# Dilated attention: two heads run among the query-key slabs, two among parts of three output slabs

## The chip, the cores and the metric

One Trainium2 chip, one NeuronCore. The time is the device time of one execution in microseconds (us): 1809.47 as the median of 3 runs (1809.37 to 1809.75) of the kernel before.

## What is computed

A two-layer block (x of 256 tokens by 1024, even mixer, odd mixer, each with a gated feed-forward part) and behind it a second two-layer block. The change touches only the odd mixer of the first block:

```python
z = h @ w_in
lru_x, lru_gate, q, k, v = jnp.split(z, [LRU_WIDTH, 2 * LRU_WIDTH, 2 * LRU_WIDTH + DIL_QKV, 2 * LRU_WIDTH + 2 * DIL_QKV], axis=-1)
xc = causal_dwconv(lru_x, lru_conv_w) + lru_conv_b
y_lru = rg_lru(xc, lru_wa, lru_ba, lru_wx, lru_bx, lru_lam) * jax.nn.gelu(lru_gate)
y_att = dilated_attention(q, k, v, q_norm_g, k_norm_g)
return jnp.concatenate([y_lru, y_att], axis=-1) @ w_out
```

`rg_lru` makes two sigmoid gates r and i from xc, a = exp(-8 r softplus(-lam)), the factor sqrt(1 - a*a), and a scan over the tokens. `dilated_attention` has 4 heads of 64 channels and, for each head, 3 patterns of (window, dilation): (128, 1), (512, 4), (2048, 16). Queries and keys are normalised to unit mean square over the 64 channels; the outputs of the 3 patterns are weighted by the softmax of their log-sums, which is one softmax over all the keys of the three patterns together.

## The kernel before

**Slabs.** All large products go through slabs: 256 output channels by 1024 (for the output projection 768) inputs of float32 weight. SyncE loads a slab's two halves into `w_raw` (three slots). ScalarE rounds each half to float32r, `w_hi` (`weights_hi`, L1149), which has three slots too: `done(slab)` (L1160) waits until TensorE has finished a slab and then rounds the slab three ahead into its slot. GpSimd or VectorE forms the rest, `w_lo = w_raw - w_hi` (`split_lo`, L471), two slabs ahead (`SPLIT_AHEAD`). TensorE multiplies in three passes for each 128 inputs: hi times hi, lo times hi, hi times lo (`passes`), 24 matmuls per half of 1024 inputs, 48 per slab, into one of four PSUM banks `lin[number % 4]`. `slab_products` (L696) makes channels by tokens, `slab_tokens` (L721) tokens by channels (for the values). Each engine has its own list of instructions, written out by hand and in order, and they meet only at semaphores.

**The odd mixer.** The order of TensorE is: 4 slabs `od_lru`, 6 slabs `od_qk` (each 128 query and 128 key channels), 3 slabs `od_v`, 4 slabs `od_out` of 768 inputs. A channel chunk of 128 holds two heads of one pattern; the chunks 0, 2, 4 are heads 0, 1 of the three patterns and 1, 3, 5 heads 2, 3.

- Query-key norm, for slab n: ScalarE squares (`qk_square`, L1355), TensorE takes the mean over 64 channels with one float32 matmul of 512 columns (`qk_mean`, L896; it writes all of `stat`, so it waits until root n-1 is out), ScalarE takes the root (`qk_root`, L1364), VectorE the reciprocal and two multiplies that also free the slab's bank (`qk_norm`, L1852). In the list of TensorE, `qk_mean(n-1)` stands behind slab n.
- The recurrence: TensorE makes the gate logits (`lru_gate`, L903) behind slabs 1 and 3, ScalarE the sigmoids, tanh and exp (L1374 to L1385, inside the loop over the slabs), VectorE the products, the scan and the gating (L1868 to L1897).
- Attention runs in 8 units, u = 2 * head + token half (`at_logits`, L927, `at_mask`, L1874, `at_exp`, L1399, and the loops L945 to L980, L1409 to L1424, L1898 to L1910). A unit is: logits (3 matmuls of 64 rows) into `logit`; VectorE scales and masks into `score`, and takes the maximum; ScalarE exp with its sum; VectorE reciprocal and scaling; TensorE 3 or 6 transposes into `tr` (and `stat`); ScalarE copies them to `pt1`; TensorE 3 or 6 value products into a bank of `lin` that is not yet in use; ScalarE copies the result into `acc`. For units 1 to 4 TensorE also lays 6 matmuls of `out_0`, the first output slab, on the recurrence's four chunks ahead of the transposes.
- Behind the last unit ScalarE rounds `acc` (both chunks, L1426), VectorE makes its low part, and TensorE does the last two chunks of out_0 (`late_part`, L760) and the slabs out_1 to out_3 (`closing`, L770). In the loop of the units the transposes and the value products of u stand where the line of dots is:

```python
for u in range(2 * DIL_H):
    if u + 2 < 2 * DIL_H:
        at_logits(u + 2)
    if 1 <= u <= 4:
        late_part(out_0, out_operand, range(k, k + NC4 // 2), OUT_LAST, wait_out_chunk, (half,))
    ...
late_part(out_0, out_operand, range(NC4, OUT_LAST + 1), OUT_LAST, wait_out_chunk)
closing([slab_at("od_out", j) for j in range(1, 4)], out_operand, None)
```

**The residual and the next norm.** As each output slab ends, ScalarE's `residual` (L1181) rounds the slab three ahead, waits for VectorE's add into x (`add_residual`, L1654), writes the gained chunks twice (rounded and not) and their squares; GpSimd's `residual` (L554) splits a half of the slab two ahead, makes the low parts of the first four chunks, and adds squares; VectorE's list has the other split halves and the low parts of the last four chunks. The first slab of the feed-forward part (`gained_products`, L789) starts with those chunks, and `norm_mean` (L741, one mean over all channels) stands behind it; from there the feed-forward slabs follow.

**DMA.** SyncE issues the halves of all slabs in slab order, each when `w_raw`'s slot is free.

## Time and profile before

| | |
|---|---|
| runs, median (lowest to highest) | 1809.47 us (1809.37 to 1809.75) |
| the profiled execution | 1810.56 us |
| its span, first to last instruction | 1808.7 us |
| mean granted TensorE clock | 0.987 |
| TensorE matmul busy | 1731.5 us, 96% of the span |
| VectorE, ScalarE, GpSimd busy | 1362.1, 1020.6, 677.7 us |

How to read it: a row of a timeline has the start from the span's beginning, the duration, the engine, the line, the operation, the names written and read, and how many instructions it merges; in brackets stands the idle time of the engine just before, and what ended it. PE is TensorE's matmul, PEld its weight load, DVE VectorE, ACT ScalarE, POOL GpSimd, SP SyncE. Matmuls overlap in the pipeline: one of 256 columns is drawn 0.28 us long and the next starts 0.12 us after it. The granted clock is the share of 2.4 GHz that TensorE had; 0.5 is 1.2 GHz.

### The profile page before, as it was taken

To read this page: it belongs to the slowest core of one execution; us is meant where nothing else is said; L and a number is where in the kernel's file an instruction comes from. 1 tells how busy PE (TensorE), PEld (TensorE's weight loads), DVE (VectorE), ACT (ScalarE), POOL (GpSimd) and SP (SyncE) were. 2 spreads that over 40 slices of the span, in tenths; PEclk is the share of its full clock that TensorE was granted. 3 is DMA by queue.
4 is the path that set the end of the run, shared out by engine and by line. 5 is a ranking of instruction groups with operands and counts; after the bars stand their busy time and mean duration, and the time that the engine had idled before them with its cause. 6 is when DMAs were issued, how large, how long until landed. Compare 5 with 4: busy or idle time off the path is not lost. (4 is left out here: it accounts for less than half of the span.)

```text
span 1808.7 us, 33606 instructions
## 1 busy us (share of the span) xinstructions
PE 1731.5 (96%) x13858; PEld 1686.1 (93%) x13858; DVE 1362.1 (75%) x1967; ACT 1020.6 (56%) x1571; POOL 677.7 (37%) x417
## 2 busy tenths in 40 slices
PE   6989999997999999999999999999999998999997
PEld 6989999986999999999889999999999888999997
DVE  5758875474686859994779589778997578769794
ACT  5465555673654564576663566546367565366462
POOL 6631104950310265344454501038334355331113
PEclk9999999998999999999999999999999999999999
DMA  7435645531455554454234455555354333545552
GB/s 268 151 112 180 201 166 176 195 114 35 146 188 185 168 189 152 163 182 143 99 125 164 163 174 196 178 176 186 129 176 163 117 116 130 176 152 196 187 173 85
DMA packets 80649, 288.42 MB, mean 159 GB/s; under 512 B 9072, under 2 KB 9328, under 8 KB 80368
## 3 DMA queue, kind: packets, MB, share of 16 engines
q1 hardware_dynamic: 79488, 283.15, 46.8%
q10 hardware_dynamic: 1008, 3.11, 0.5%
q8 instruction: 110, 1.80, 0.4%
q14 instruction: 43, 0.35, 0.1%
HBM read 285.18 MB, written 1.05 MB: 158 GB/s over the span
## 5 line engine op out<-in xcount | busy, mean ns | idle before, releaser
L1157 ACT ACTIVATE w_hi<-w_raw 128x1024 fp32r<-128x1024 f32 (+1 forms) x546 | 538.0, 1033 | 337.0 <-PE lin L677 336.0
L477 POOL TENSOR_TENSOR w_lo<-w_raw,w_hi 128x1024 fp32r<-128x1024 f32 (+1 forms) x198 | 476.9, 2420 | 360.9 <-ACT w_hi L1157 355.2
L675 PE MATMUL lin<-h_hi,w_hi 128*128 128x256 f32 x1952 | 560.6, 287 | 24.3 <-DVE w_lo L477 18.3
L675 PE MATMUL lin<-hid_hi,w_hi 128*128 128x256 f32 x1936 | 553.5, 286 | 10.5 <-DVE hid_lo L486 7.2
L676 PE MATMUL lin<-h_lo,w_hi 128*128 128x256 f32 x1952 | 555.3, 284 | 0.0
L677 PE MATMUL lin<-h_hi,w_lo 128*128 128x256 f32 x1952 | 555.2, 284 | 0.0
L676 PE MATMUL lin<-hid_lo,w_hi 128*128 128x256 f32 x1936 | 548.6, 283 | 0.0
L677 PE MATMUL lin<-hid_hi,w_lo 128*128 128x256 f32 x1936 | 548.5, 283 | 0.0
L477 DVE TENSOR_TENSOR w_lo<-w_raw,w_hi 128x1024 fp32r<-128x1024 f32 (+1 forms) x348 | 495.1, 1426 | 36.9 <-ACT w_hi L1157 35.9
L675 PEld LDWEIGHTS lin<-h_hi,w_hi 128*128 128x128 f32 x1952 | 377.7, 194 | 26.5 <-issue 17.5
L675 PEld LDWEIGHTS lin<-hid_hi,w_hi 128*128 128x128 f32 x1936 | 372.2, 192 | 13.3 <-DVE hid_lo L486 6.1
L676 PEld LDWEIGHTS lin<-h_lo,w_hi 128*128 128x128 f32 x1952 | 377.8, 194 | 0.8 <-issue 0.5
L677 PEld LDWEIGHTS lin<-h_hi,w_lo 128*128 128x128 f32 x1952 | 377.6, 193 | 0.0
L676 PEld LDWEIGHTS lin<-hid_lo,w_hi 128*128 128x128 f32 x1936 | 372.4, 192 | 0.3
L677 PEld LDWEIGHTS lin<-hid_hi,w_lo 128*128 128x128 f32 x1936 | 372.3, 192 | 0.0
L1691 DVE SCALAR_TENSOR_TENSOR acc<-arena,par,acc 128x254 f32<-128x254 f32 (+1 forms) x264 | 156.4, 632 | 3.0
L486 POOL TENSOR_TENSOR h_lo<-arena,h_hi 128x256 fp32r<-128x256 f32 x48 | 36.3, 764 | 279.5 <-ACT h_hi L1215 219.2
L486 POOL TENSOR_TENSOR hid_lo<-arena,hid_hi 128x256 fp32r<-128x256 f32 x48 | 36.3, 762 | 258.6 <-ACT hid_hi L1215 219.2
L1669 DVE TENSOR_TENSOR x<-x,lin 128x512 f32<-128x512 f32 x64 | 43.8, 685 | 100.8 <-PE lin L677 100.8
L1705 DVE TENSOR_TENSOR arena<-lin,std 128x512 f32<-128x512 f32 x88 | 60.7, 690 | 60.5 <-PE lin L677 60.3
L1227 ACT ACTIVATE acc<-arena,par 128x256 f32<-128x256 f32 x88 | 48.3, 596 | 93.8 <-DVE arena L1705 93.8
L1223 ACT ACTIVATE acc<-arena,par 128x256 f32<-128x256 f32 x44 | 26.5, 603 | 112.1 <-DVE arena L1705 112.1
(307 smaller groups left out, 2148.3 us busy)
## 6 DMA issues: line engine op xcount, KB each, us to landing
w_raw<-in_upA SPq DMA_DIRECT2D x112, 512.0 KB, 3.6
w_raw<-in_upB SPq DMA_DIRECT2D x64, 512.0 KB, 4.2
w_raw<-in_xbc SPq DMA_DIRECT2D x48, 512.0 KB, 4.1
w_raw<-in_dnA SPq DMA_DIRECT2D x32, 512.0 KB, 3.5
w_raw<-in_dnB SPq DMA_DIRECT2D x32, 512.0 KB, 3.4
w_raw<-in_z SPq DMA_DIRECT2D x32, 512.0 KB, 4.1
w_raw<-in_gates SPq DMA_DIRECT2D x32, 512.0 KB, 3.8
w_raw<-in_ps SPq DMA_DIRECT2D x32, 512.0 KB, 4.0
```

Source lines behind the costliest of these rows:

```text
L477: eng.tensor_tensor(w_lo[slab.slot][:, half, part], w_raw[slab.slot][:, half, part], w_hi[slab.slot][:, half, part].bitcast(F32), ALU.subt ...
L486: return eng.tensor_tensor(lo, whole, hi.bitcast(F32), ALU.subtract)
L675: nc.tensor.matmul(out, lhs[0], rhs[0], start=first, stop=False)
L676: nc.tensor.matmul(out, lhs[0], rhs[1], start=False, stop=False)
L677: return nc.tensor.matmul(out, lhs[1], rhs[0], start=False, stop=last)
L1157: nc.scalar.activation(w_hi[slab.slot][:, half, part], w_raw[slab.slot][:, half, part], ACT.Copy)\
L1223: nc.scalar.activation(acc[:, b, 0, :], zz[:, j, 0, :], ACT.Identity, bias=pcol(f"fb{f}", c), scale=pcol(f"fw{f}", 2 * FC + c)).then_inc(s ...
L1227: ins = nc.scalar.activation(acc[:, b, i, :], zz[:, j, i, :], ACT.Identity, bias=pcol2(l, "fb", i * FC + c), scale=pcol2(l, "fw", 2 * 2 * ...
L1669: tt(pairs[:, j, :, :], pairs[:, j, :, :], lin[slab.bank][:, :, :], ALU.add)\
L1691: ins = stt(outs[i][:, d:T], ins_[i][:, 0:T - d], weight(taps - 1 - d, i), outs[i][:, d:T], ALU.mult, ALU.add)
L1705: tt(zz[:, j, :, :], lin[slab.bank][:, :, :], std[:, 0, 0:T].unsqueeze(1).to_broadcast([P, 2, T]), ALU.mult).then_inc(s.bank_free[slab.ban ...
```

## The change

The arrays of weights are cut anew: the q-k slabs come in the order of chunks 0, 2, 4, then 1, 3, 5 (`od_qa`, `od_qb`), the values by head pair (`od_va` with head 0, `od_vb` with the others), and between them the order of slabs is `od_qa` 3, `od_va` 1, `od_qb` 3, `od_vb` 2, `od_out` 4. Units 0 to 3 (heads 0, 1) run among the slabs of `od_qb` and `od_vb`, in the middle of a slab too (`between`), with their value products written to `tr`. Units 4 to 7 run among parts of out_0, out_1 and out_2, whose first four chunks are laid between the steps of the units, the chunk of heads 0, 1 next, and the chunk of heads 2, 3 behind the last unit. The lists of ScalarE and VectorE are written out anew to match; the high and low part of the attention's output are made per chunk (`att_round`, `att_rest`). GpSimd splits both halves of out_2. Cut to its core:

```diff
+QK_ORDER = (0, 2, 4, 1, 3, 5)
...
-         ("od_lru", 4), ("od_qk", 6), ("od_v", 3), ("od_out", 4),
+         ("od_lru", 4), ("od_qa", 3), ("od_va", 1), ("od_qb", 3), ("od_vb", 2), ("od_out", 4),
...
+        def at_product(u):
+            lo = 64 * (u // 2 % 2)
+            return (tr if u < UNITS // 2 else lin[slab_at("od_out", 3).bank][:, 0, :])[lo:lo + 64, 0:P]
...
+                    if k < both:
+                        split_lo(pool, slab_at(stage, k, l).ahead(SPLIT_AHEAD), 1)
...
+            residual("od_out", 3, both=1)
...
+            slab_products(qk_slabs[0], h_op(1))
+            stage_released(pe, "od_lru")
+            pe.wait_ge(s.lru_first, 2)
+            lru_gate(0)
+            slab_products(qk_slabs[1], h_op(1))
+            qk_mean(0)
+            pe.wait_ge(s.lru_r, 1)
+            lru_gate(1)
+            slab_products(qk_slabs[2], h_op(1))
+            qk_mean(1)
+            slab_tokens(v_slabs[0], 1, lambda: qk_mean(2))
+            slab_products(qk_slabs[3], h_op(1))
+            at_logits(0)
+            slab_products(qk_slabs[4], h_op(1), between=lambda: at_logits(1))
+            at_transposes(0)
+            qk_mean(3)
+            def first_values():
+                at_values(0)
+                at_logits(2)
+            slab_products(qk_slabs[5], h_op(1), between=first_values)
+            at_transposes(1)
+            def second_values():
+                at_values(1)
+                at_logits(3)
+                qk_mean(4)
+            slab_tokens(v_slabs[1], 1, second_values)
+            at_transposes(2)
+            qk_mean(5)
+            slab_tokens(v_slabs[2], 1)
+            at_transposes(3)
...
+            def out_part(j, chunks, halves=(0, 1)):
+                for half in halves:
+                    if chunks[0] == 0:
+                        outs[j].wait_split(pe, half)
+                        if half == 0:
+                            outs[j].wait_bank_free(pe)
+                    late_part(outs[j], out_operand, chunks, OUT_LAST, wait_out_chunk, (half,))
...
+            out_part(0, from_lru, (0,))
+            at_values(2)
+            out_part(0, from_lru, (1,))
+            at_values(3)
+            at_logits(4)
+            out_part(1, from_lru)
+            at_logits(5)
+            out_part(2, from_lru, (0,))
+            at_transposes(4)
+            out_part(2, from_lru, (1,))
+            at_values(4)
+            at_logits(6)
+            out_part(0, lower_heads)
+            at_transposes(5)
+            out_part(1, lower_heads)
+            at_values(5)
+            at_logits(7)
+            out_part(2, lower_heads)
+            for u in (6, 7):
+                at_transposes(u)
+                at_values(u)
+            for j in range(3):
+                out_part(j, upper_heads)
+            closing(outs[3:], out_operand, None)
...
+            done(qk_slabs[0])
+            qk_square(0)
+            lru_sigmoid(0, lru_r, "lru_ba", s.lru_r)
+            done(qk_slabs[1])
+            qk_square(1)
+            qk_root(0)
+            lru_sigmoid(1, lru_i, "lru_bx", s.lru_i)
+            done(qk_slabs[2])
+            qk_square(2)
+            act.wait_ge(s.lru_r, 1)
+            act.wait_ge(s.lam_chain, LAM_LINKS)
+            for func, out in ((ACT.Tanh, lru_th), (ACT.Exp, lru_a)):
+                for c in range(NC4):
+                    ins = nc.scalar.activation(out[:, c, :], lru_r[:, c, :], func, scale=small[:, c:c + 1])
+            ins.then_inc(s.lru_a, 1)
+            qk_root(1)
+            qk_root(2)
+            v_copy(0)
+            act.wait_ge(s.lru_m2, 1)
+            nc.scalar.activation(lru_th[:, :, :], lru_m[:, :, :], ACT.Sqrt, scale=-1.0).then_inc(s.lru_mult, 1)
+            done(qk_slabs[3])
+            qk_square(3)
+            at_exp(0)
+            at_exp(1)
+            at_turned(0)
+            done(qk_slabs[4])
+            qk_square(4)
+            at_copy(0)
+            qk_root(3)
+            act.wait_ge(s.lru_y, 1)
+            nc.scalar.activation(raw_set(1)[0][:, 0:NC4, :], lru_hs[:, :, :], ACT.Copy).then_inc(s.lru_y_hi, 1)
+            at_exp(2)
+            at_turned(1)
+            done(qk_slabs[5])
+            qk_square(5)
+            at_copy(1)
+            qk_root(4)
+            at_turned(2)
+            qk_root(5)
+            at_exp(3)
+            v_copy(1)
+            v_copy(2)
+            at_turned(3)
+            at_copy(2)
+            at_copy(3)
+            att_round(0)
+            at_exp(4)
+            at_exp(5)
+            at_turned(4)
+            at_copy(4)
+            at_exp(6)
+            at_turned(5)
+            at_copy(5)
+            at_exp(7)
+            for u in (6, 7):
+                at_turned(u)
+                at_copy(u)
+            att_round(1)
...
-                    if k < COUNT[stage] - late:
+                    if k < COUNT[stage] - late and (stage, k) != ("od_out", 0):
...
+            qk_norm(0)
+            dve.wait_ge(s.lru_i, 1)
+            stage_released(dve, "od_lru")
+            dve.wait_ge(s.lru_first, 2)
+            lc.link(tt(lru_i[:, :, :], lru_i[:, :, :], lru_xc[:, :, :], ALU.mult))
+            qk_norm(1)
+            dve.wait_ge(s.lru_a, 1)
+            lc.link(tt(lru_m[:, :, :], lru_a[:, :, :], lru_a[:, :, :], ALU.mult))
+            stt(lru_m[:, :, :], lru_m[:, :, :], 1.0, lru_th[:, :, :], ALU.add, ALU.mult).then_inc(s.lru_m2, 1)
+            qk_norm(2)
+            dve.wait_ge(s.lru_mult, 1)
+            lc.link(tt(lru_i[:, :, :], lru_i[:, :, :], lru_th[:, :, :], ALU.mult))
+            at_mask(0)
+            for c in range(NC4):
+                ins = nc.vector.tensor_tensor_scan(lru_hs[:, c, :], lru_a[:, c, :], lru_i[:, c, :], 0.0, ALU.mult, ALU.add)
+            lc.link(ins)
+            at_mask(1)
+            at_probs(0)
+            tt(lru_hs[:, :, :], lru_hs[:, :, :], lru_gate[:, :, :], ALU.mult).then_inc(s.lru_y, 1)
+            at_probs(1)
+            at_mask(2)
+            qk_norm(3)
+            at_probs(2)
+            dve.wait_ge(s.lru_y_hi, 1)
+            lo_part(nc.vector, raw_set(1)[1][:, 0:NC4, :], lru_hs[:, :, :], raw_set(1)[0][:, 0:NC4, :]).then_inc(s.lru_y_lo, 1)
+            at_mask(3)
+            qk_norm(4)
+            at_probs(3)
+            qk_norm(5)
+            at_mask(4)
+            at_mask(5)
+            att_rest(0)
+            at_probs(4)
+            at_mask(6)
+            at_probs(5)
+            at_mask(7)
+            at_probs(6)
+            at_probs(7)
+            att_rest(1)
+            dve.wait_ge(s.w_lo[1], slab_at("od_out", 3).number)
```

The parts are, in this order: the stages, the place of the value products, GpSimd's split, and the lists of TensorE, ScalarE and VectorE. New waits inside the steps: `at_logits(0)` waits for the banks of the three `od_qa` slabs, that is for `qk_norm(2)`; `at_logits(4)` for those of `od_qb`; `at_transposes(u)` for the copy of the values of the unit before where both use `tr`; `qk_mean(4)` for the second copied transposes.

## Rows read from the trace of the kernel before

**Rows 1.** Windows: length, busy us (instructions) of PE, PEld, DVE, ACT, POOL; PEclk; DMA share, GB/s

```profile
326.00:480.00 154.00, 138.72 (x984) 127.25 (x983) 83.47 (x102) 90.72 (x153) 79.19 (x40) 0.93 0.36 115
480.00:790.00 310.00, 305.97 (x2528) 304.60 (x2527) 253.84 (x379) 170.05 (x258) 101.23 (x63) 1.00 0.53 176
...
396.40:399.70 3.30, 3.30 (x18) 3.30 (x17) 3.27 (x4) 2.02 (x4) 3.30 (x3) 0.51 0.43 119
...
413.40:430.40 17.00, 12.91 (x47) 10.23 (x48) 6.94 (x11) 5.80 (x14) 1.81 (x1) 0.50 0.09 31
...
440.00:455.30 15.30, 9.94 (x70) 7.60 (x68) 5.74 (x12) 6.61 (x17) 0.00 (x0) 1.00 0.00 0
```

**Rows 2.** Waits of TensorE, 345 to 480 us: us in total, times, longest us

```profile
PE logit L934 <- ACT arena L1391: 3.9, 1, 3.9
PE lin L976 <- ACT arena L1418: 3.8, 4, 1.0
PE lin L976 <- ACT sq L1416: 2.7, 4, 1.0
PE stat L900 <- ACT std L1368: 1.9, 1, 1.9
PE lin L675 <- DVE hid_lo L486: 1.8, 1, 1.8
```

**Rows 3.** Timeline, TensorE, 356 to 477 us

```profile
356.54 1.02 PE L900 MATMUL stat<-arena,cst 128*128 128x512 f32 x2
357.39 1.89 PE L906 MATMUL logit<-arena 128*128 128x256 f32 x8
...
437.87 1.52 PE L976 MATMUL lin<-arena 128*64 128x128 f32 x12 [0.96 <-ACT arena L1418]
...
442.88 1.56 PE L934 MATMUL logit<-arena 64*128 64x256 f32 x6
...
455.29 0.39 PE L675 MATMUL lin<-hid_hi,w_hi 128*128 128x256 f32 x1 [1.75 <-DVE hid_lo L486]
...
476.64 1.89 PE L748 MATMUL stat<-sq,cst 128*128 128x256 f32 x8
```

**Rows 4.** Timeline, VectorE, the add behind two feed-forward slabs

```profile
501.60 0.69 DVE L1705 TENSOR_TENSOR arena<-lin,std 128x512 f32<-128x512 f32 x1 [1.03 <-PE lin L677]
...
507.36 0.69 DVE L1705 TENSOR_TENSOR arena<-lin,std 128x512 f32<-128x512 f32 x1 [1.03 <-PE lin L677]
```

**Rows 5.** Timeline, ScalarE, 385 to 395 us

```profile
385.83 1.71 ACT L1385 ACTIVATE arena<-arena,small 128x256 f32<-128x256 f32 x4
...
390.46 2.00 ACT L1157 ACTIVATE w_hi<-w_raw 128x1024 fp32r<-128x1024 f32 x2
...
392.96 1.28 ACT L1368 ACT_TABLE_LOAD   x1
394.25 0.69 ACT L1368 ACTIVATE std<-stat,eps 128x512 f32<-128x512 f32 x1
```

**Rows 6.** Timeline, VectorE, recurrence, norms, and unit 6's mask to the next scaling

```profile
390.66 1.23 DVE L1871 TENSOR_TENSOR arena<-arena 128x1024 f32<-128x1024 f32 x1 [2.16 <-ACT arena L1385]
...
395.13 3.34 DVE L1855 RECIPROCAL std<-std 128x512 f32<-128x512 f32 x1
...
399.30 3.34 DVE L1855 RECIPROCAL std<-std 128x512 f32<-128x512 f32 x1
...
445.35 0.96 DVE L1882 SCALAR_TENSOR_TENSOR arena<-logit,arena 128x768 f32<-128x768 f32 x1 [1.87 <-PE stat L968]
...
447.40 0.42 DVE L1902 TENSOR_SCALAR arena<-arena,small 128x384 f32<-128x384 f32 x1
```

**Rows 7.** Timeline, ScalarE, GpSimd and VectorE behind out_0

```profile
457.03 1.58 ACT L1157 ACTIVATE w_hi<-w_raw 128x768 fp32r<-128x768 f32 x2 [2.52 <-PE lin L677]
...
461.35 1.87 POOL L477 TENSOR_TENSOR w_lo<-w_raw,w_hi 128x768 fp32r<-128x768 f32 x1
...
466.27 3.32 DVE L477 TENSOR_TENSOR w_lo<-w_raw,w_hi 128x1024 fp32r<-128x1024 f32 x1
```

More of the change, by code:

```diff
@@ L618, in _ @@
             opening("od_lru", 1)
-            weights("od_qk", both=True)
-            weights("od_v", both=True)
-            residual("od_out", 3)
+            for stage in ("od_qa", "od_va", "od_qb", "od_vb"):
+                weights(stage, both=True)
+            residual("od_out", 3, both=1)
             ffn(1, 4)
@@ L694, in tile_of, with slab_products @@
                 return w_hi[slab.slot][:, half, part], w_lo[slab.slot][:, half, part]
-            def slab_products(slab, rhs, waits=(None, None)):
+            def slab_products(slab, rhs, waits=(None, None), between=None):
                 slab.wait_bank_free(pe)
@@ L701, in slab_products @@
                 for half in range(2):
+                    if half == 1 and between is not None:
+                        between()
                     slab.wait_split(pe, half)
@@ L726, in slab_tokens @@
                 for t in range(2):
+                    if t == 1 and between is not None:
+                        between()
                     out = lin[slab.bank][:, t, :].rearrange("p (a b) -> p a b", a=2)
@@ L969, in _ @@
                 mm.then_inc(s.at_tr, 1)
-                pe.wait_ge(s.at_pt, u + 1)
-                if u >= 2:
-                    pe.wait_ge(s.at_out, u - 1)
-                for b in range(nb):
-                    g, st = b // (t + 1), b % (t + 1)
-                    v_at = (g * DIL_H + head) * DIL_D
-                    mm = nc.tensor.matmul(at_bank[u % 2][lo:lo + 64, 0, 0:P], vt[:, st, v_at:v_at + DIL_D],
-                                          pt1[u % 2][:, b * P:b * P + P], start=(b == 0), stop=(b == nb - 1))
@@ L978, in _, with at_values @@
-                mm.then_inc(s.at_pv, 1)
-            late_part(out_0, out_operand, range(NC4, OUT_LAST + 1), OUT_LAST, wait_out_chunk)
-            closing([slab_at("od_out", j) for j in range(1, 4)], out_operand, None)
+            def at_values(u):
+                head = u // 2
+                pe.wait_ge(s.at_pt, 4 if u == 2 else u + 1)
+                if u >= 1:
+                    pe.wait_ge(s.at_out, u)
+                if u % 2 == 0 and u < 6:
+                    v_slabs[u // 2].wait_released(pe)
+                blocks = at_blocks(u)
+                for b, g, st in blocks:
+                    v_at = (head * DIL_G + g) * DIL_D
+                    mm = nc.tensor.matmul(at_product(u), vt[:, st, v_at:v_at + DIL_D],
+                                          pt1[u % 2][:, b * P:b * P + P], start=(b == 0), stop=(b == len(blocks) - 1))
+                mm.then_inc(s.at_pv, 1)
```

188 lines of the change are left out of this document (67 added, 121 removed).

## Prediction

> **What bounds the kernel now.** I read the windows by stage first [rows 1]. The odd mixer, 326 to 480 us, has TensorE busy for 138.72 of 154.00 us at a mean granted clock of 0.93; the feed-forward part behind it has 305.97 of 310.00 at 1.00. So TensorE sets the pace nearly everywhere, and this stage alone leaves room. The same windows show where the clock stood at its lower level of 1.2 GHz: 396.4 to 399.7 us (0.51) and 413.4 to 430.4 us (0.50). The waits of TensorE from 345 to 480 us come next [rows 2]: 3.9 for a copied value slab, 3.8 and 2.7 for turned probabilities, 1.9 for a root, 1.8 for the last low part, 14.1 in all. The first clock fall follows the wait of 1.9, the second begins inside that of 3.9. Last, starts in order of time [rows 3]: the first q-k mean at 356.54, so the first q-k slab ended one slab (5.76) earlier, at 350.8; the products behind the last head unit at 455.29; the next norm's mean at 476.64. From there TensorE runs on without a wait, so whatever moves 476.64 moves the end one for one. The kernel's last chain lies elsewhere and is not touched.
>
> **Account of the old order, 350.8 to 455.3.** A slab is 48 matmuls in 5.76 us, seen from VectorE's adds behind two slabs at 501.60 and 507.36 [rows 4]; one matmul is 0.12. Of the small groups the last 0.1 lies beside the next, so I take from rows 3 q-k mean 0.85 (356.54 to 357.39), gate 1.7 (1.89 long), and for the second token half logits 1.45 (1.56 long) and values 1.45 (1.52 long, 12 matmuls); the first half streams half the columns or half the matmuls, 0.8 each; transposes are three and six such matmuls, 0.4 and 0.7. Work: 8 slabs 46.1, 6 means 5.1, 2 gates 3.4, four heads of logits 9.0, transposes 4.4, values 9.0, and 24 matmuls of out_0 2.9: 79.9 of 104.5 us. The other 24.6 are the 14.1 of waits, 1.6 for the short fall, and 8.5 for the long one (half of 17.0), which gives 24.2.
>
> **The new order's work.** The same, plus 48 matmuls of out_1 and out_2 and 18 for heads 0, 1: 90 matmuls instead of 24, 10.8 us. Sum 87.8. So 7.9 us of products move from behind the last unit to ahead of it. What decides is how much waiting stays, and I walked the four engines' new lists with these durations.
>
> (a) *q-k mean 2, in the middle of the first value slab.* TensorE: 350.8, gate, slab, mean, gate, slab: slab 2 is done at 366.6; mean 1 and half a slab more, 370.3. Mean 2 needs root 1 out of stat. ScalarE from 366.8: high part of a slab 2.0, square 0.5 (what lies between 392.46 and the load at 392.96), tanh 1.65 (1.71 long, as is exp), table load 1.28, exp 1.65, table load 1.28, root 0.7 [rows 5]: 375.8. **Wait 5.5.**
>
> (b) *Logits 0 need q-k norm 2.* VectorE from 375.9: a norm 4.2 (reciprocal to reciprocal, 395.13 to 399.30); then a*a and the product behind it, 4.5 (390.66 to 395.13; a*a alone is 1.23, and GpSimd splits beside the product in both orders); then another norm 4.2: 388.8 [rows 6]. TensorE ended slab 3 at 385.3. **Wait 3.5.**
>
> (c) Transposes 0 stand behind the scan, mask 1 and its maximum: wait 1.2. From there to the last value slab everything that a unit waits for lies beside 2.88 us of slab, and I cost it at nothing; if VectorE (three reciprocals there) ran some 3 us late, that cover would be gone. (d) Values 2 stand behind four roundings of out_1 and out_2 and two copies on ScalarE: 1.0.
>
> (e) *Units 4 to 7.* VectorE's scaling of unit u stands behind the mask of u+1, which needs its logits. Unit 6: logits 7 end at 448.9, and mask, maximum, reciprocal and scaling take 2.5 (445.35 to 447.82) [rows 6]: 451.5. TensorE has 6 matmuls, 0.7, to lay beside that: wait 1.9. The others by the same reckoning: 1.5, 1.3, 0.3, 0.6, 1.0. Sum 6.6. (f) Behind values 7: copy, high part, low part, now of one chunk: 1.5 instead of 1.75.
>
> Waits 5.5 + 3.5 + 1.2 + 1.0 + 6.6 + 1.5 = 19.3. 350.8 + 87.8 + 19.3 = **457.9, against 455.3**: the last unit ends 2.6 later.
>
> **Behind the last unit.** Old: 120 matmuls, 14.4, to 469.7; then 6.9 to the mean at 476.64. New: 18 matmuls, 2.2, to 460.1, then out_3. But there are three weight slots and out_0 to out_2 fill them. The rounding of out_3 begins when out_0 is done; its low part, first half, is behind ScalarE's gained chunks and GpSimd's two low parts. Old: rounding starts 457.03, that split ends 463.22 [rows 7]: 6.2 us, hidden by out_1 and out_2 (8.6). New: out_0 is done at 458.8, so 465.1: **wait 5.0**. Then out_3, 4.3: 469.4. The 6.9 stay: ScalarE starts 1.8 later on the same four slabs' work, but finds them done, where it used to wait for TensorE between them. So 476.3, **-0.3**. One split of 1.87 [rows 7] moves from VectorE to a GpSimd that idles there; SyncE issues the same transfers for the same slab numbers, and no wait in rows 2 is for a transfer: both nothing.
>
> **The clock.** The old trace fell after 1.9 of waiting, so I expect falls at (a), (b) and ahead of out_3. Each of the short kind (3.3 us) costs 1.65 if nothing absorbs it. The first is absorbed by (b). The second loses 0.5 beyond (c). The third I put at 0.9, since the next slab's splits are late too (0.7). Together 1.4; bounds 0 (no fall) and 6 (each twice as long, none absorbed). The old long fall is not added back: its 8.5 are in the 24.6.
>
> **Table loads.** By its list ScalarE switches tables seven times here in the old order and ten times in the new. The trace has 1.28 for one, and the activation behind it starts 0.02 later, 392.96 to 394.25 [rows 5]; three more are inside (a) to (e). The Trainium skill (ScalarE: Activation LUTs, What ACT_TABLE_LOAD costs) gives 1.28 and a drain of 1.38 for every switch. By that (a) would be 2.8 longer and the sum about +4; the trace shows no drain, so I go by the row.
>
> **Sum.** -0.3 + 1.4 = +1.1. The profiled execution took 1810.56 (span 1808.7), 1.09 above the median 1809.47; against the median: **1810.6**. Less than 0.2% (3.6 us, about what a measurement of this kernel tells from no change). Bounds from the walk itself: the same reckoning of the old order puts its last unit 0.1 to 1.6 late, depending on how VectorE and GpSimd take turns (the split of 3.32 in rows 7, which overlaps one of GpSimd's).
>
> **Rivals.**
> 1. *The waits (a) and (b) do not come.* For: the old order had 1.9 at its worst before the units [rows 2]. Against: both are sums along one engine's own list. Both gone is -9.0; what is then late is VectorE's work for units 0 to 3, whose three norms (4.2 each) lose their slack, so I return a third: -6, 1804.6. Better still if units 4 to 7 are also covered: 1799. Chance 0.15.
> 2. *Slower: the clock stays low in units 4 to 7.* Place: 438 to 458. Of 20 us some 13.9 are TensorE's work; at 1.2 GHz they cost 13.9 more, of which the 6.6 of waits take back most: +8, 1818.6. It decides if the clock falls at a wait of under 2 us there. For: the fall after 1.9. Against: 440.0 to 455.3 has waits of 1.0 to 1.75 with TensorE busy 9.94 of 15.30 and the clock stayed at 1.00 [rows 1]. Chance 0.12.
> 3. *Slower, by late splits*: VectorE's operands from SBUF and GpSimd's splits take turns wrongly in 385 to 400 or behind out_3 (in the old order one split took 3.32 [rows 7]): two such turns, +4, 1814.6. Chance 0.13.
> 4. The forecast, 1807 to 1813: 0.60.
>
> **How the numbers follow.** Faster by over 0.2% is rival 1, 0.15; slower is rivals 2 and 3, 0.25; within, 0.60. The range takes in rival 3 and the clock's upper bound (1816.6) and rival 1's nearer price: 1804.5 to 1817.0.
>
> **What would show it.** Right: a wait of 4 to 6 us before the third q-k mean for a root, 2 to 4 before the first logits for VectorE, 4 to 6 before out_3 for GpSimd's low part; the last unit's products start 1 to 4 us later than 455.3 on the old scale; table loads ten. Wrong: if the first two waits are missing, rival 1; if the granted clock is near 0.5 between the last value slab and the last values, rival 2; if SyncE's transfers are what anyone waits for, I missed a queue. The forecast fails if the mean of the next norm starts over 3.6 us from 476.6.

## The result, and the profile after

The changed kernel took 1818.33 us, median of five executions from 1813.85 to 1819.92; the kernel before beside it 1809.43 (1809.13 to 1809.75). The ratio is 1.0043, with an interval of 1.0032 to 1.0053: slower by 0.4%, where 1810.6 and "within 0.2%" were forecast. The forecast's range ended at 1817.0. The executions of the changed kernel also lie 6 us apart, where the five of the old one lie 0.6 apart (the 28 that ran beside the last experiments lie 4.9 apart, 1807.05 to 1811.93). A second batch of the unaltered changed kernel (after_again, below) has a median of 1816.74, with a ratio of 1.0041: the slowing repeats, at a size just inside the forecast's range.

The windows of the changed kernel's profiled execution (1819.92 us, span 1818.1), in the form of [rows 1] but for TensorE alone: length, busy us (instructions), granted clock, DMA share, GB/s. The first two are the stage and the feed-forward part behind it.

```profile
326.00:488.00 162.00, 142.34 (x984) 0.92 0.35 109
488.00:798.00 310.00, 305.97 (x2516) 0.99 0.53 175
375.20:382.10 6.90, 6.18 (x23) 0.51 0.08 31
399.10:402.50 3.40, 3.40 (x10) 0.51 0.00 0
440.00:457.00 17.00, 12.18 (x86) 1.00 0.00 0
457.30:467.40 10.10, 7.87 (x35) 0.50 0.01 2
470.90:477.60 6.70, 5.79 (x27) 0.50 0.52 167
```

The stage, cut at the same distance behind the next norm's mean as in [rows 1], is 8 us longer and has 3.6 us more of busy TensorE for the same 984 matmuls. Four stretches stand at 1.2 GHz, 27 us in all; in the old order there were two, of 3.3 and 17 us.

The waits of TensorE from 345 to 486 us, the view of [rows 2]:

```profile
PE tr L962 <- DVE arena L1998: 6.2, 4, 2.2
PE stat L917 <- ACT std L1440: 5.5, 1, 5.5
PE lin L686 <- POOL w_lo L486: 4.0, 1, 4.0
PE lin L686 <- DVE hid_lo L495: 1.3, 1, 1.3
PE lin L976 <- ACT arena L1468: 1.2, 2, 1.0
PE tr L976 <- ACT arena L1468: 0.9, 1, 0.9
PE lin L976 <- ACT sq L1466: 0.6, 1, 0.6
```

That is 19.7 us, against 14.1 in the old order. And where they stand, in the timeline of TensorE that answers to [rows 3]:

```profile
350.68 1.89 PE L923 MATMUL logit<-arena 128*128 128x256 f32 x8
...
375.92 1.19 PE L917 MATMUL stat<-arena,cst 128*128 128x512 f32 x1 [5.54 <-ACT std L1440]
...
388.38 0.37 PE L938 MATMUL logit<-arena 64*128 64x128 f32 x1
...
399.10 0.47 PE L962 MATMUL tr<-cst,arena 128*128 128x128 f32 x1 [2.19 <-DVE arena L1998]
...
430.05 0.32 PE L976 MATMUL tr<-sq,arena 128*64 128x128 f32 x1 [0.91 <-ACT arena L1468]
...
455.33 0.33 PE L962 MATMUL tr<-cst,arena 128*128 128x128 f32 x1 [1.66 <-DVE arena L1998]
...
459.79 0.47 PE L976 MATMUL lin<-arena 128*64 128x128 f32 x1 [0.96 <-ACT arena L1468]
...
463.88 0.58 PE L686 MATMUL lin<-hid_hi,w_hi 128*128 128x256 f32 x1 [1.27 <-DVE hid_lo L495]
...
471.81 0.55 PE L686 MATMUL lin<-hid_hi,w_hi 128*128 128x256 f32 x1 [3.97 <-POOL w_lo L486]
...
484.52 1.89 PE L763 MATMUL stat<-sq,cst 128*128 128x256 f32 x8
```

The first row is the gate at the end of q-k slab 0. Then: mean 2, logits 0, transposes 0, values 2, transposes 6, values 7, the first products behind the last unit, out_3, the next norm's mean. The last stands 7.9 us later than in [rows 3]; the span is 9.4 longer, and the rest is one more fall of 3.4 us in the part behind (743.9 to 747.3) and smaller differences.

**How the runs are compared below.** The clock also falls near 95 us, far ahead of the change, for 3.4 us in some executions and 6.8 or 10.2 in others, and that moves everything behind it by some 3 us. So all places are given as a distance from G, the end of q-k slab 0: the start of the first gate in the new order (350.68 here), the first q-k mean less one slab of 5.76 in the old (350.8). E is the distance to the first output products behind the last unit, M that to the next norm's mean. "Slow" is the time at 1.2 GHz between G and M, from windows as above.

| kernel | E | M | slow | median us | ratio to before, interval |
|---|---|---|---|---|---|
| before | 104.5 | 125.9 | 20.6 | 1809.4 | |
| changed | 113.2 | 133.8 | 27.4 | 1818.3 | 1.0043, 1.0032 to 1.0053 |
| after_again (the same) | 110.4 | 130.0 | 20.4 | 1816.7 | 1.0041, 1.0029 to 1.0053 |
| fill_late | 108.4 | 127.4 | 6.8 | 1809.2 | 1.0012, 1.0001 to 1.0022 |
| fill_late_again (the same) | 108.4 | 127.5 | 6.8 | 1812.9 | 1.0023, 1.0013 to 1.0033 |
| tail_fill | 110.4 | 130.0 | 13.6 | 1816.8 | 1.0036, 1.0022 to 1.0050 |
| all_fill | 111.0 | 130.0 | 3.5 | 1812.3 | 1.0023, 1.0014 to 1.0032 |
| two_open | 110.9 | 129.9 | 17.0 | 1814.3 | 1.0033, 1.0020 to 1.0045 |
| one_open | 113.2 | 135.6 | 37.5 | 1821.5 | 1.0063, 1.0049 to 1.0077 |
| root1_first | 108.9 | 129.7 | 24.0 | 1812.7 | 1.0020, 1.0011 to 1.0028 |
| root1_fill | 104.4 | 123.4 | 0 | 1808.4 | 0.9991, 0.9982 to 1.0000 |
| root1_two_fill | 106.1 | 125.1 | 10.3 | 1810.2 | 1.0003, 0.9994 to 1.0012 |
| old_fill | 98.2 | 119.5 | 0 | 1803.8 | 0.9966, 0.9953 to 0.9979 |
| old_two | 98.3 | 118.5 | 0 | 1801.8 | 0.9958, 0.9946 to 0.9971 |

E, M and slow are of the one profiled execution, which need not be one near the median; the median is of all. One of the five executions of one_open took 8114.02 us; it is in that median and not in the ratio.

### The profile page after: what moved, and what is told of

Read it like the earlier page. It is cut to its first block, busy times and chain, and to the rows that moved or that the text cites. A ratio compares the mean times of both kernels' runs of the same rounds, so it can differ in the third digit from the quotient of the medians.

```text
span 1818.1 us, 33628 instructions
## 1 busy us (share of the span) xinstructions
PE 1737.5 (96%) x13858; PEld 1691.9 (93%) x13858; DVE 1363.1 (75%) x1967; ACT 1023.7 (56%) x1575; POOL 676.9 (37%) x418
## 4 chain that ended last, share of the span: by engine, by line
PE 38%; DVE 18%; ACT 4%; issue 2%; POOL 0%; DVEq 0%; ACTq 0%
PE lin L686 12%; PE lin L688 12%; PE lin L687 12%; DVE w_lo L486 4%; DVE acc L1804 3%; DVE arena L2287 1%; ACT w_hi L1232 1%; DVE arena L2114 1%; DVE stat L2065 1%; DVE sq L2228 1%; ACT sq L1643 1%; DVE arena L2124 1%; PE tr L1150 1%; ACT L1643 1%; DVE std L2284 1%
```

## The experiments

Two theories at the start. C: the walk of the new order was about right, and the clock takes what is missing. W: the clock's falls lie beside waits, and the order itself is longer than reckoned. Two helpers make matmuls whose results change nothing: `keep_busy` starts constant products in a free bank (0.45 us each, and the profile counts each as two instructions), `add_nothing` adds products with a weight of zeros into out_0's bank.

**1. Fill the late waits (fill_late), and the same for the long wait of the old order (old_fill).**

```diff
+            add_nothing(outs[0], 12)
             at_transposes(6)
+            add_nothing(outs[0], 4)
             at_values(6)
             at_transposes(7)
+            add_nothing(outs[0], 7)
             at_values(7)
+            add_nothing(outs[0], 10)
...
+            outs[3].wait_bank_free(pe)
+            keep_busy(outs[3], 9)
             closing(outs[3:], out_operand, None)
```

> The changed kernel, with matmuls that add nothing in places where TensorE waits late in the attention: 12, 4, 7 and 10 products by a weight of zeros, accumulated into out_0's bank (ahead of transposes 6, values 6, transposes 7 and behind values 7), and nine constant matmuls of some 0.4 us into out_3's free bank ahead of the three closings' end. Theory C (the clock's falls at 457 to 467 and 471 to 478 us cost the time; the new waits by themselves are short): the granted clock stays at 1.00 from 403 to 500, the products behind the last unit start near 460.5 instead of 463.9, the next norm's mean near 479 to 480 instead of 484.5, the median is 1812 to 1813.5 and the runs of one kernel lie closer together. Rival W (the order's own waits and the late split of out_3 hold the time, the falls lie beside them): the mean stays within 1 us of 484.5, the time at 1817 to 1819.

```diff
             at_logits(1)
+            out_0.wait_bank_free(pe)
+            keep_busy(out_0, 8)
             stage_released(pe, "od_v")
```

> The kernel before, with eight constant matmuls of some 0.4 us (3.4 us, results not used) into out_0's free bank between logits 1 and the last value slab's release, where TensorE waits 3.9 us and the clock falls for 17 us. Theory C (what the long fall of the old order costs is real time, about half of it absorbed by the units' waits): no fall at 413 to 430, the products behind the last unit start at 448 to 450 instead of 455.3, the median is 1802 to 1804. Rival (units 0 to 3 are paced by the chain over VectorE, ScalarE and GpSimd, the fall lies beside it): the products still start at 454 to 455.5, the median is 1808 to 1809.5.

TensorE's timeline and one window of fill_late:

```profile
348.00 0.38 PE L923 MATMUL logit<-arena 128*128 128x256 f32 x1
...
449.84 0.55 PE L972 MATMUL tr<-cst,arena 128*128 128x128 f32 x3 [0.24 <-DVE arena L2015]
...
456.40 0.39 PE L686 MATMUL lin<-hid_hi,w_hi 128*128 128x256 f32 x1
...
458.66 4.04 PE L945 MATMUL lin<-cst 128*128 128x256 f32 x18
...
463.67 0.35 PE L686 MATMUL lin<-hid_hi,w_hi 128*128 128x256 f32 x1 [0.97 <-POOL w_lo L486]
...
475.43 1.89 PE L763 MATMUL stat<-sq,cst 128*128 128x256 f32 x8
```

```profile
451.00:463.00 12.00, 11.57 (x77) 10.08 (x77) 3.44 (x6) 7.42 (x15) 2.66 (x3) 1.00 0.00 1
```

The clock stays at 2.4 GHz behind the fall at mean 2. M is 127.4, 6.4 less than in the changed kernel (on its scale the mean stands at 478.1, a little better than theory C's 479 to 480), and the median is 1809.2 where 1812 to 1813.5 was expected. One part of the expectation missed: the executions did not draw together. Seven of twelve took 1808.2 to 1809.3 and five 1815.3 to 1816.0. The same kernel run again had a median of 1812.9, so M, which repeats (127.45), is the surer number here. The wait ahead of out_3 is now whole, 4.04 of filler and 0.97 behind it: 5.0 us.

In old_fill the fall of 17 us is gone, and so is the short one of 3.3 us, which stood ahead of the filler and by itself moved logits 2 by only 0.3 (65.2 behind G in the kernel before, 64.8 here). The rows, of its TensorE:

```profile
353.37 0.59 PE L900 MATMUL stat<-arena,cst 128*128 128x512 f32 x1
...
408.79 0.92 PE L930 MATMUL lin<-cst 128*128 128x256 f32 x3
...
445.81 0.39 PE L675 MATMUL lin<-hid_hi,w_hi 128*128 128x256 f32 x1 [1.75 <-DVE hid_lo L486]
```

E falls from 104.5 to 98.2 (449.0 on the scale of before, as theory C had it), M by 6.3, and the median to 1803.76 (expected 1802 to 1804; the profiled execution, 1800.78, is one of two that took 1800.5 to 1800.8, the other three took 1803.8 to 1804.9). So 20 us at half clock cost the old order 6.3 us and the new one about as much. **With these falls taken out of both, the new order is still 7.9 behind the old (127.4 against 119.5).** The fall at mean 2 is still in the 127.4, but it costs little there: the norm that logits 0 need ends 36.0 behind G, and logits 0 start at 36.5; with that fall filled too (all_fill, below) VectorE is ready for transposes 0 no earlier, 47.8 against 47.2. Theory C explains why the forecast missed, but not why the new order is slower than the old.

**2. Two slabs open (two_open), one slab open (one_open), a filler ahead of out_3 alone (tail_fill).**

```diff
-            out_part(2, from_lru, (0,))
             at_transposes(4)
-            out_part(2, from_lru, (1,))
...
-            out_part(2, lower_heads)
...
-            for j in range(3):
+            for j in range(2):
                 out_part(j, upper_heads)
-            closing(outs[3:], out_operand, None)
+            closing(outs[2:], out_operand, None)
```

> The changed kernel with two output slabs held open instead of three: out_2 is done whole behind the last unit, ahead of out_3, as are its 48 matmuls. Theory (the wait of 4.0 us ahead of out_3 comes from three weight slots filled by three open slabs, so that out_3's low part begins only when out_0 is done): the wait ahead of out_3 is under 0.5 us, no clock fall at 471 to 478, products behind the last unit up to 2 us earlier, 3 to 5 us of out_2 go back behind them; the next norm's mean at 480 to 482 instead of 484.5; median 1813 to 1816. Rival (what is behind the last unit is set by the vector engines' splits and not by the slots): the mean within 1 us of 484.5, median 1817.5 or more.

The mean came at 480.6 on the changed kernel's scale and the median at 1814.26, both as expected; but the wait for GpSimd's low part only shrank to 1.29 us, and the clock fell in the units all the same.

one_open leaves out out_1's parts too.

> The changed kernel with one output slab held open, as in the old order: heads 0 and 1 still run amid the query-key slabs, but out_1 and out_2 are done whole behind the last unit. So this is the first half of the change alone. Theory (waits in units 4 to 7 take back what is no longer laid beside them): the wait ahead of transposes 4 and 6 rises to 3 us or more each, no wait ahead of out_3, products behind the last unit at 107 to 110 us behind the gate, the next norm's mean at 129 to 131, median 1812 to 1816. Rival (the heads amid the slabs gain by themselves and only the open slabs cost): the mean at or under 126 behind the gate, median at or under 1809.

tail_fill has only the last two added lines of fill_late.

> The changed kernel with only the nine constant matmuls (some 4 us, results not used) in the wait ahead of out_3, nothing in units 6 and 7. If the two falls are separate prices: the fall at 457 to 467 stays and with it the late products behind the last unit (113 us behind the gate of q-k slab 1, as in the changed kernel), the fall at 471 to 478 is gone, the next norm's mean comes 132 to 133 us behind that gate instead of 133.8; median 1814 to 1817. If instead the fall behind the last unit follows from the one ahead of it, both go or both stay, and the mean is either below 130 or at 133.5 and above.

one_open, windows and the wait ahead of transposes 4:

```profile
437.30:467.90 30.60, 23.30 (x91) 0.50 0.00 0
```

```profile
437.01 0.76 PE L962 MATMUL tr<-cst,arena 128*128 128x128 f32 x3 [2.90 <-DVE arena L1993]
```

The waits ahead of transposes 4 and 6 rose to 2.9 and 2.6, nearly the expected 3; then the clock stayed at 1.2 GHz for 30.6 us, all of units 4 to 7, E and M are beyond what was expected, and the median is 1821.5, the slowest of all. So heads 0 and 1 amid the slabs, with one slab open and the clock as it then falls, are worse than the whole change; what they would bring at full clock no run shows. In tail_fill M is 130.0 where 132 to 133 was expected, yet not by the filler: after_again has the same 130.0 without it (below). From E to M tail_fill takes 19.7 us with no fall ahead of out_3, after_again 19.7 with one of 3.4 us and the changed kernel 20.6 with one of 6.8: a short fall in that wait is free, a long one costs 1.0. The fall in units 6 and 7 costs 2.0 (E 110.4 in both against 108.4 in fill_late). In the changed kernel's own profiled execution E is another 2.8 later, and that was lost before those units (below).

**3. ScalarE's root ahead of the tanh (root1_first).**

```diff
             qk_square(2)
+            qk_root(1)
             act.wait_ge(s.lru_r, 1)
...
             ins.then_inc(s.lru_a, 1)
-            qk_root(1)
             qk_root(2)
```

> The changed kernel with ScalarE's root of q-k slab 1 moved ahead of the tanh and the exp of the block before it, directly behind the square that it needs (one table load of 1.28 us more). Theory (the wait of 5.5 us before q-k mean 2 is that chain and costs time): the wait goes to 1.0 to 2.0 us, the clock does not fall at 375 to 382, slab 3 ends about 4 us earlier, and part of it, up to 4 us, reaches the end: 1814 to 1816. Rival (what comes next, the scan ahead of transposes 0, is late anyway): the wait before transposes 0 grows by what the first one lost, the mean of the next norm moves by less than 1 us, 1817 to 1820.

The wait before mean 2 went from 5.54 to 0.95, logits 0 now waited 1.59 for VectorE, and M is 4.2 less than the changed kernel's 133.8, with 24.0 us at half clock against 27.4, though only 0.3 less than after_again's 130.0. Free of that scatter is the start of transposes 0: 43.3 behind G here and in root1_fill, 47.3 in fill_late and 47.4 in after_again, so 4.0 earlier. The median, 1812.73, is better than 1814 to 1816. The chain (a) costs real time, and one more table load of 1.28 us pays for its removal.

**4. Every wait filled (all_fill), the late ones and the root together (root1_fill), and that with two slabs open (root1_two_fill).**

```diff
+            def third_mean():
+                qk_slabs[3].wait_bank_free(pe)
+                keep_busy(qk_slabs[3], 12)
+                qk_mean(2)
-            slab_tokens(v_slabs[0], 1, lambda: qk_mean(2))
+            slab_tokens(v_slabs[0], 1, third_mean)
...
+            qk_slabs[5].wait_bank_free(pe)
+            keep_busy(qk_slabs[5], 4)
             at_transposes(0)
```

> The changed kernel with matmuls that add nothing in all its long waits: 12 constant ones (5.2 us) ahead of q-k mean 2, four (1.7 us) ahead of transposes 0, and those of the earlier run in units 6 and 7 and ahead of out_3. Theory: with no fall left from 360 to 480 us the profiled execution shows the new order's price without the clock: products behind the last unit 107 to 108.5 us behind the gate of q-k slab 1, the next norm's mean at 126.5 to 128, median 1807.5 to 1810, and the second group of runs near 1815.5 is gone. That is still 7 us behind the old order with its one wait filled (119.5 behind the gate, 1803.8): then waits and not the clock make most of the difference between the orders. Rival (the remaining runs near 1815 come from falls elsewhere, or the fillers delay the vector engines' chain): the second group stays, or the median is above 1811.

This missed, for the reason that its rival names. VectorE and GpSimd in all_fill:

```profile
378.26 8.04 POOL L486 TENSOR_TENSOR w_lo<-w_raw,w_hi 128x1024 fp32r<-128x1024 f32 x3 [8.37 <-ACT w_hi L1255]
378.37 3.38 DVE L2037 SCALAR_TENSOR_TENSOR arena<-arena 128x1024 f32<-128x1024 f32 x1
```

and TensorE's logits 0 behind them:

```profile
386.07 0.90 PE L938 MATMUL logit<-arena 64*128 64x128 f32 x6 [3.37 <-DVE arena L1994]
```

The same two in fill_late:

```profile
378.62 1.22 DVE L2031 SCALAR_TENSOR_TENSOR arena<-arena 128x1024 f32<-128x1024 f32 x1
...
380.16 4.77 POOL L486 TENSOR_TENSOR w_lo<-w_raw,w_hi 128x1024 fp32r<-128x1024 f32 x2 [10.00 <-ACT w_hi L1249]
```

With the wait at (a) filled, the half slab behind it runs at 2.4 GHz, ScalarE's rounding and GpSimd's split start earlier, and the split begins 0.11 us ahead of a VectorE product that then takes 3.38 us instead of 1.22. The Trainium skill (SBUF — State Buffer, SBUF: two separate sides) says that GpSimd and a VectorE instruction with two SBUF inputs take one port pair by turns, each for its whole instruction; the trace agrees: the first of GpSimd's three splits (8.04 in all) takes 2.40, and had 2.29 left to run when the product began; the delay is 2.16. Logits 0 then start 38.3 behind G instead of 36.5. Behind their wait of 3.37 the clock falls for 3.4 us, and logits 1 are 3.2 late; the former wait ahead of transposes 0 takes 2.2 of that, but the four matmuls laid into it, 1.7 us, now have no wait to stand in. Transposes 0 start 49.9 behind G instead of 47.3: that is the 2.6 by which M is worse than in fill_late. So the turn alone is not the cause; the fall and the filler behind it have their part. The second group of executions stayed as well (1816.7 to 1818.3, four of eleven).

root1_fill is fill_late with the moved root and the four matmuls ahead of transposes 0.

> The changed kernel with the earlier fillers (units 6 and 7, ahead of out_3), four constant matmuls more ahead of transposes 0, and ScalarE's root 1 moved ahead of the tanh and exp. It asks how much of the new order's loss that is not the clock's comes from ScalarE's list at the third mean. Theory: values 2, which stood 76.6 us behind the gate of q-k slab 1 with the late fillers alone and at 74.1 with the root moved and one fall of 3.4 us, come at 72 to 73.5, the next norm's mean at 123 to 124.5, median 1804.5 to 1806.5. Rival (units 4 to 7 and the split of out_3 are paced by the vector engines' lists from the start): the mean stays at 126.5 or more, median 1808 or more.

root1_two_fill takes out_2's parts out of that, as in two_open, and the filler ahead of out_3.

> The same with two output slabs held open instead of three and no filler ahead of out_3. Theory: 30 matmuls fewer ahead of the last unit bring 3.6 us and give back 1.9 in longer waits ahead of transposes 4 and 6, and the 5.0 us ahead of out_3 become two waits of 1.3: the mean 121.5 to 123 us behind the gate, median 1803 to 1805, still above the old order with its wait filled and two slabs open (1801.75). Rival (the clock falls in the longer waits of units 4 to 6, which have no fillers): the time lies at 1807 or more.

Values 2 of root1_fill stand at 72.6 behind G and M at 123.4, both as expected, with no slow stretch between. The median missed (1808.4, expected at most 1806.5): in the profiled execution the clock fell for 10.2 us near 95, before the change begins; the two quickest took 1804.7 and 1805.6. In root1_two_fill the rival was right: the clock fell from 430.5 to 440.8, M is 125.1 and the median 1810.2. Transposes 4 start 84.85 behind G in both kernels, with 12 matmuls, 1.4 us, less ahead of them in the second, where TensorE waits 2.90 instead of 1.28: VectorE's chain sets that moment, and what is laid ahead of it is free. The two kernels differ by the fall as well, so they do not tell which number of open slabs is better at full clock.

**5. The old order with a second slab open (old_two).** Added to old_fill:

```diff
                 mm.then_inc(s.at_tr, 1)
+                if 2 <= u <= 5:
...
+                    half, k = (u - 2) // 2, (u - 2) % 2 * (NC4 // 2)
+                    late_part(out_1, out_operand, range(k, k + NC4 // 2), OUT_LAST, wait_out_chunk, (half,))
                 pe.wait_ge(s.at_pt, u + 1)
```

> The kernel before with the eight constant matmuls in its long wait, and with a second output slab held open: the 24 matmuls of out_1's first four chunks (2.9 us) stand six each between transposes and values of units 2 to 5, where TensorE waits 0.6 to 1.0 us for turned probabilities. Theory (what stands in a wait of about its own length is free): the unit waits fall from 6.5 us in total by some 2.5, the last unit ends within 0.7 us of where it did, 2.9 us leave the part behind it, out_3 waits 0.5 for its low part; mean 117 to 118.5 us behind the same gate instead of 119.5, median 1801 to 1803. Rival (what is laid there pushes the chain of logits, mask and scaling back by its own length): the last unit ends 2.5 us later, median 1803.5 to 1805.

```profile
432.38 0.87 PE L991 MATMUL lin<-sq,arena 128*64 128x128 f32 x6
...
436.51 0.76 PE L991 MATMUL lin<-arena 128*64 128x128 f32 x5 [0.25 <-ACT arena L1434]
...
445.59 0.39 PE L675 MATMUL lin<-hid_hi,w_hi 128*128 128x256 f32 x1 [1.75 <-DVE hid_lo L486]
...
453.63 0.36 PE L675 MATMUL lin<-hid_hi,w_hi 128*128 128x256 f32 x1 [0.58 <-POOL w_lo L477]
...
465.73 1.89 PE L748 MATMUL stat<-sq,cst 128*128 128x256 f32 x8
```

In TensorE's rows above, values 4 wait for nothing now (0.58 before) and values 5 0.25 (0.96). E is 98.3 as against 98.2, so 24 matmuls were laid ahead of the last unit for 0.1 us; the wait of 0.6 ahead of out_3 came as reckoned. M 118.5, median 1801.75, both as expected. This version beats both kernels: 0.9958 of the kernel before. That it also beats old_fill rests on M (1.1 less); the medians differ by 2.0, less than old_fill's own executions do.

**6. The same kernels again (after_again, fill_late_again).**

> The changed kernel once more, unaltered, beside the same runs of the kernel before as the other experiments. Its own executions lay between 1813.9 and 1819.9 us. Expected if the length of the clock's falls makes that spread: the order of the instructions and every wait for another engine stay as they were, and the profiled execution's time goes with the summed length of its stretches at 1.2 GHz (after: 51 us of them before the last stage, time 1819.9), about half a microsecond for one, less where a wait absorbs it. If the spread comes from the vector engines or transfers instead, waits of TensorE for them change by microseconds. Median 1814 to 1819.

> The kernel with the late fillers once more, unaltered: seven of its twelve executions took 1808.2 to 1809.3 us, five 1815.3 to 1816.0, with nothing between. If the profiled execution is of the second group, its trace shows what the 6.5 us are: by the theory a longer stretch or more stretches at 1.2 GHz, some 13 us of them, in a place that the profiled one of the first group had at 2.4 GHz; by the rival, the same clock and one wait of 6 us for another engine. If it is of the first group, nothing is told.

The changed kernel again has its waits to within 0.2 us (5.54, 2.20, 0.91, 1.28, 1.06, 1.66, 3.77), and a profiled execution of 1812.07 us, 7.85 less than the first. Over the whole span but its last stage it had 37 us at 1.2 GHz instead of 55: 0.46 us of time for each. The fall at transposes 0 did not come, that at units 6 and 7 did. So the same instructions fall in one execution and not in another. In the eleven executions of the two batches the mean granted clock goes with the time, from 0.988 for the two of 1812 us to 0.983 for the four of 1818.3 to 1819.9. That the falls make the spread is shown for the two that were profiled, and fits the rest.

The profiled execution of fill_late_again (1808.94) has the falls, E and M of the first, so it tells nothing of the slower ones. Its batch fills the gap, though: 1812.1, 1812.9, 1812.9 and 1813.7 lie between the two groups of the first batch, at a clock of 0.990, and 1815.2 and 1816.2 are at 0.988, where the quick ones have 0.991. Where the slower executions lose their time stays open.

## Why the forecast was wrong, step by step

- **The work and its place: right.** The same 984 matmuls in the stage, 90 of the open slabs ahead of the last unit. Table loads went from seven to ten, as listed.
- **(a) the third mean: right, 5.54 against 5.5.** The trace of ScalarE has the chain as it was summed:

```profile
370.78 1.28 ACT L1495 ACT_TABLE_LOAD   x1
372.07 0.51 ACT L1495 ACTIVATE arena<-arena,small 128x256 f32<-128x256 f32 x1
...
373.79 1.28 ACT L1440 ACT_TABLE_LOAD   x1
375.09 0.69 ACT L1440 ACTIVATE std<-stat,eps 128x512 f32<-128x512 f32 x1
```

  The activation begins 0.01 to 0.02 us behind each load. The Trainium skill (ScalarE: Activation LUTs, What ACT_TABLE_LOAD costs) adds a drain of 1.38 to every switch; by that the wait would have been some 2.8 longer, and the trace disagrees.
- **(b) logits 0: right at full clock, absent as a wait in the changed kernel.** With (a) filled it is there, 3.37 against 3.5, and so is the split beside the product that the reckoning took from the old order (3.38 long, 3.28 there). In the changed kernel the half clock behind (a) delays that split, the product runs alone, and the norm ends at 386.71, where 388.8 was reckoned:

```profile
381.31 1.23 DVE L2014 SCALAR_TENSOR_TENSOR arena<-arena 128x1024 f32<-128x1024 f32 x1
...
386.23 0.48 DVE L1971 SCALAR_TENSOR_TENSOR arena<-lin,par,std 128x256 f32<-128x256 f32 x1
```

  Logits 0 start at 388.38 because TensorE itself, at half clock, is not there before. That this is near the 388.8 reckoned for VectorE is luck.
- **(c) transposes 0: 2.2 against 1.2.** VectorE took 3.23 us for a product of the kind that takes 1.2 alone, and 5.59 for the scan that took 2.44 in old_fill, where no split ran; both stood beside GpSimd splits, the turns of rival 3:

```profile
386.62 3.23 DVE L2017 TENSOR_TENSOR arena<-arena 128x1024 f32<-128x1024 f32 x1
...
390.95 5.59 DVE L2020 TENSOR_TENSOR_SCAN arena<-arena 128x256 f32<-128x256 f32 x4
```

```profile
384.01 4.76 POOL L486 TENSOR_TENSOR w_lo<-w_raw,w_hi 128x1024 fp32r<-128x1024 f32 x2 [11.18 <-ACT w_hi L1232]
```

  In fill_late the two differences cancel: by the prediction's terms transposes 0 start 47.2 behind G (38.0 for logits 0, then 0.8, 2.9, 1.45, 2.9 and the wait of 1.2), and they start at 47.26, though logits 0 stand at 36.5.

- **(d), (e), (f): right.** 0.9 against 1.0; in units 4 to 7 1.3, 1.1, 0.25, 1.7, 0.6 and 1.0, 5.8 in all, against 6.6; 1.3 against 1.5.
- **The end of the last unit without the clock: 108.4 (fill_late), reckoned 107.1.** Transposes 0 being in place, the 1.3 lies behind them: in fill_late the stretches from there on are up to 0.5 longer than their terms (values 2 to transposes 4 take 12.3, 11.8 by the terms). The groups were priced a little too short; the same reckoning of the old order had left 0.4 open.
- **Behind the last unit: 19.0 without the clock, reckoned 18.4.** The wait of 5.0 ahead of out_3 was exact, for the reason given: out_3 is rounded only when out_0 has freed its slot, and GpSimd's low part follows.
- **The clock: this is the step that failed.** It was put at 1.4: the first fall absorbed by (b), the second 0.5, the third 0.9, and none elsewhere. The profiled execution lost 6.4 (M 133.8 against 127.4 with the late waits filled), the second one 2.6. Three falls came about where they were named (the second at (c) and not at (b)), two of them 6.9 and 6.7 us long where 3.3 was taken; the fourth, 457 to 467 us, was not named. Against fill_late the 6.4 are:
  - 1.2 at the fall behind (a). It ended 31.4 behind G, in fill_late 28.8; ScalarE's rounding and GpSimd's split came 1.2 later, and with them the end of VectorE's product (3.23 against 2.07) that transposes 0 stand behind (48.4 against 47.3 behind G). Logits 0, 37.7 behind G, are still within the 38.0 reckoned, so the slack of (b) did cover TensorE; it did not cover the splits.
  - 1.6 at the fall at (c), 399 to 402.5 (values 0 are 2.8 late in all, 54.3 against 51.5). It did not come in after_again.
  - 2.0 in units 6 and 7, in both executions. This fall begins behind waits of 1.66 and 0.58 in unit 6. It was put at nothing, because in [rows 1] the old order kept its clock over waits of 1.0 to 1.75 just there.
  - 1.6 ahead of out_3, where 0.9 was taken (0.6 in after_again, whose fall there was 3.4 us long).
- **The fall in units 6 and 7 is rival 2's mechanism in half its place**, to which I gave 0.12, and a quarter of its price: 2.0 us, not 8. That the median, 1818.33, is next to rival 2's 1818.6 is luck. The fall was no accident of one execution: there is one in unit 6 or 7 in all six traces of the new order without fillers there (changed, after_again, tail_fill, two_open, one_open, root1_first), while all three traces of the old order (before, old_fill, old_two) kept the clock in their last units. What in the new order makes the difference no run here shows. Nor do such waits absorb a fall as I let rival 2's do: a wait for turned probabilities is 0.58 or 0.96 at either clock (in the kernel before at 419 us, at half clock, and at 433), since TensorE's own transposes stand in the chain.
- **The outer bound was mis-summed.** "Each twice as long, none absorbed" is three times 3.3, 9.9 us, and not 6. The measured 6.4 lies beyond the stated bound and inside the one that the words give.
- **The sum of errors** for the profiled execution, up to the mean: walk 1.3, clock ahead of the last unit 4.8 where 0.5 was taken, walk behind it 0.6, clock behind it 1.6 where 0.9 was taken, together 6.9 beyond the forecast +1.1. That is the 7.9 seen. A further 1.5 lies behind the mean.
- **What the forecast did not ask.** The long fall of the old order was left in the 24.6 us of waits and half clock, and was never priced apart. Both falls together were worth 6.3 us (old_fill), 6.0 of it behind logits 2, where the long one lies. The change was sized against an order that itself lost as much to the clock, and so its own loss of 7.9 could not be seen as one.

**Where the 7.9 lie.** Moving root 1 takes 4.0 of them away (M from 127.4 to 123.4; this is also the step at which transposes 0 come 4.0 earlier). The rest compares root1_fill and old_fill, neither of which has a fall. With it moved, 66 more matmuls (7.9 us) stand ahead of the last unit, and it ends only 6.2 later (104.4 against 98.2): 1.7 is gained. Behind it 7.9 less work brings only 2.3 (19.0 against 21.3), because of the 5.0 us ahead of out_3: 5.6 is lost. The balance, 3.9, is the other half. This is a reckoning from two traces; no run took the wait of 5.0 away and left all else. Whether out_3 could be split earlier with a fourth weight slot was not tried.

## What to carry to other kernels

Price every stretch at half clock as a cost of its own, in the kernel before too: ask what the order would take at full clock, and fill one wait with matmuls that add nothing to measure it. Work that is laid into a wait is free up to the wait's length and on that engine alone; holding a third slab open filled waits of 1 to 3 us but used the last weight slot, and against the old order the new one gained 1.7 ahead of the last unit and lost 5.6 behind it, most of that in the wait of 5.0. A VectorE instruction beside a GpSimd split took up to 2.2 us more than alone, so a chain's price depends on what moves the splits. Where a change multiplies short waits, compare more than one profiled execution: the list of waits repeats to 0.2 us, the clock does not.

## What the runs showed that I had not expected

- A filler can cost time: matmuls laid in the wait for mean 2 brought the next split 1.6 us forward (as a distance from G), onto a VectorE product (1.22 to 3.38 us); with the fall and the filler that followed, the next norm's mean came 2.6 later than in fill_late.
- Eight constant matmuls of 3.7 us, put where TensorE had waited 3.9, made the kernel before 5.5 us faster, 0.9966 of its time.
- The length of a fall ahead of the change (3.4 us, or 6.8 to 10.2, near 95 us) moved the whole stage by some 3 us from one execution of the same code to the next; a row's absolute time is no measure of the change until that is taken out.
